# Second attention: forget sums and low queries in one product, value parts in one weight tile per head

## The reference

```python
log_f = jax.nn.log_sigmoid(f_logit + b_forget)
cum_log_f = jnp.cumsum(log_f, axis=1).transpose(0, 2, 1)
z = einsum('bhtd,bhsd->bhts', q, k) / 8 + cum_log_f[..., t] - cum_log_f[..., s]
z = where(s <= t, z, -1e30)
y_b = einsum('bhts,bhsd->bhtd', softmax(z), v)
y_b = (y_b * silu(z_b)) @ w_o_fox
```

## Time and profile before

| | before |
|---|---|
| median of 3 runs | 1290.13 us (1289.41 to 1290.8) |
| profiled execution, span from first to last instruction | 1286.8 us |
| TensorE busy | 1254.0 us (97%) |
| VectorE busy | 758.9 us (59%) |
| ScalarE busy | 586.3 us (46%) |
| GpSimd busy | 748.3 us (58%) |
| mean granted TensorE clock | 0.996 |

### The profile page before, as it was taken

One profiled execution on the slowest core, in us unless ns is written; L12 is line 12 of the kernel. 1 busy time (PEld: TensorE's weight loads), 2 busy tenths in 40 slices (PEclk: granted clock), 3 DMA queues, 4 the chain that ended last, 5 costly groups with the idle time before them and its releaser, 6 DMA issues.

```text
span 1286.8 us, 17060 instructions
## 1 busy us (share of the span) xinstructions
PE 1254.0 (97%) x6226; PEld 1044.0 (81%) x6226; DVE 758.9 (59%) x1245; ACT 586.3 (46%) x956; POOL 748.3 (58%) x863
## 2 busy tenths in 40 slices
PE   5999999999999999999999999999999999999997
PEld 4777878878888888887778988887888888888887
DVE  5868778334444367698787337754367616651565
ACT  3375667445664446233456644434333313331332
POOL 2644443434333676676545878535659957885782
PEclk9999999999999999999999999999999999999999
DMA  9412223222344733233224444212323333333322
GB/s 381 173 66 79 93 82 140 86 95 99 107 130 135 242 120 99 82 99 103 68 68 158 138 148 131 81 52 66 98 65 99 112 102 98 98 99 99 90 90 66
DMA packets 43107, 142.74 MB, mean 111 GB/s; under 512 B 4880, under 2 KB 7440, under 8 KB 41872
## 3 DMA queue, kind: packets, MB, share of 16 engines
q1 hardware_dynamic: 42768, 141.39, 33.6%
q10 hardware_dynamic: 256, 0.26, 0.1%
HBM read 130.88 MB, written 8.39 MB: 108 GB/s over the span
## 4 chain that ended last, share of the span: by engine, by line
PE 79%; DVE 14%; ACT 4%; issue 1%; POOL 1%; DMA 1%; SPq 0%; DVEq 0%; ACTq 0%; POOLq 0%
PE ps L124 78%; DVE tm L134 2%; DVE tm L137 2%; ACT tm L131 2%; ACT L131 1%; DVE ac L137 1%; PE ps L128 1%; DVE spl L134 1%; DVE tm L142 1%; DVE sph L145 1%; DVE x L137 1%; DVE ewl L134 1%; DMA x<-xin 1%; DVE ma L137 1%; POOL ycl L134 0%
## 5 line engine op out<-in xcount | busy, mean ns | idle before, releaser
L134 POOL TENSOR_TENSOR wl<-raw,wh 128x256 fp32r<-128x256 f32 x804 | 691.3, 892 | 480.6 <-ACT wh L131 472.7
L131 ACT ACTIVATE wh<-raw 128x1024 fp32r<-128x1024 f32 x201 | 212.0, 1055 | 310.8 <-PE ps L124 304.9
L124 PE MATMUL ps<-hh,wh 128*128 128x512 f32 x872 | 344.4, 395 | 0.0
L124 PE MATMUL ps<-hh,wl 128*128 128x512 f32 x872 | 340.2, 390 | 0.0
L124 PE MATMUL ps<-hl,wh 128*128 128x512 f32 x872 | 339.9, 390 | 0.0
L124 PEld LDWEIGHTS ps<-hh,wl 128*128 128x128 f32 x872 | 163.9, 188 | 34.9
L124 PEld LDWEIGHTS ps<-hh,wh 128*128 128x128 f32 x872 | 164.2, 188 | 33.3 <-DVE tm L137 0.4
L124 PEld LDWEIGHTS ps<-hl,wh 128*128 128x128 f32 x872 | 164.2, 188 | 32.9
L134 DVE TENSOR_TENSOR tm<-tm,tm 128x512 f32<-128x512 f32 (+4 forms) x113 | 94.3, 839 | 42.1 <-ACT tm L131 38.9
L137 DVE SCALAR_TENSOR_TENSOR tm<-cb,par_sb,tm 128x512 f32<-128x512 f32 x88 | 87.1, 990 | 50.5 <-ACT tm L131 47.1
L131 ACT ACTIVATE tm<-tm 128x512 f32<-128x512 f32 (+3 forms) x109 | 54.0, 531 | 80.5 <-DVE tm L137 64.5
(11 more groups left out here) (308 smaller groups left out, 2273.5 us busy)
## 6 DMA issues: line engine op xcount, KB each, us to landing
raw<-units SPq DMA_DIRECT2D x201, 512.0 KB, 3.5
ada<-units SPq DMA_DIRECT2D x16, 512.0 KB, 14.5
kept<-ge SPq DMA_DIRECT2D x16, 256.0 KB, 2.5
tm<-kept SPq DMA_DIRECT2D x16, 256.0 KB, 3.5
tm<-gate_w SPq DMA_DIRECT2D x12, 256.0 KB, 4.0
x<-xin SPq DMA_DIRECT2D x2, 1024.0 KB, 6.1
x<-xin SPq DMA_DIRECT2D x1, 2048.0 KB, 9.5
out<-x SPq DMA_DIRECT2D x16, 128.0 KB, 1.8
```

The source lines that it names most:

```text
L124: return self.none if self.e is None else self.e.matmul(out, lhs, rhs, start=start, stop=stop, skip_group_check=skip)
L131: return self.none if self.e is None else self.e.activation(out, in_, func, **kw)
L134: return self.none if self.e is None else self.e.tensor_tensor(out, a, b, op)
```

## The change

The one-hot rows move into the zero half of QL0, and the forget sums into a copy of the keys: KF[x] holds on one half the high keys of the head, and on the other the forget sums (high parts in 8 rows, low parts in 8 rows 32 further) and zeros. The second score product takes KF for K2, and the third is gone. VectorE writes the one-hot half behind the low queries and copies the keys behind their low parts. GpSimd zeroes both KF tiles in place of FT, later than FT was, as they lie in the first attention's value tiles.

The values of a head stand in one weight tile of 128 columns, 64 high and 64 low. Two passes, by PTh and PTl, give four parts; the result has the high values' half on partitions 0 to 63 and the low values' half on 64 to 127. ScalarE copies the latter to FO (`low_half`, last in its work for the head), VectorE adds it to the other half into the head's own half of the bank, and the gate product follows.

```diff
@@ constants @@
-        out[64 + h, o + h] = 1.0
+        for r in (32, 64, 96):
+            out[r + h, o + h] = 1.0
@@ tiles @@
+    KF = [at(f"kf{x}", [P, T], F32R, a1 + 4096 + 8192 * x + 6144) for x in range(2)]
+    VB = at("vb", [P, 4, 2 * T], F32R, vb0)
-    FT = at("ft", [P, T], F32R)
+    FO = at("fo", [64, T], F32)
+    def heads(tile, t, part):
+        return tile[:, t, :].rearrange("p (h x d) -> p h x d", h=8, x=2)[:, :, part, :]
+    def per_head(bank):
+        return bank[:, :].rearrange("p (h d) -> p h d", h=8)
@@ tensor_program, qk_b @@
+            pe.wait_ge(s_kf, c, x)
+            pe.wait_ge(s_hot, c, x)
...
-                pe.mm(PS[b][:, 0:n], QL0[p][x][:, w], K2[p][x][:, 0:n], False, False)
-                pe.mm(PS[b][:, 0:n], conr[0:72, CO + h:CO + h + 1].to_broadcast([72, 128]), FT[0:72, 0:n], False, False)
+                pe.mm(PS[b][:, 0:n], QL0[p][x][:, w], KF[x][:, 0:n], False, False)
@@ pv_b @@
-                vh, vl = (x[:, j, c * 128:(c + 1) * 128] for x in (VBh, VBl))
+                both = VB[:, j, 128 * h:128 * h + 128]
                 pe.wait_ge(s_vl, "b", j)
-                pe.mm(PS[b][:, 128 * j:T], vh, PTh[:, j, 128 * j:T], j == 0, False)
-                pe.mm(PS[b][:, 128 * j:T], vh, PTl[:, j, 128 * j:T], False, False)
-                last = pe.mm(PS[b][:, 128 * j:T], vl, PTh[:, j, 128 * j:T], False, j == 3)
+                pe.mm(PS[b][:, 128 * j:T], both, PTh[:, j, 128 * j:T], j == 0, False)
+                last = pe.mm(PS[b][:, 128 * j:T], both, PTl[:, j, 128 * j:T], False, j == 3)
@@ scalar_program @@
-                            act.wait_ge(l_mout[t // 2], 0)
+                            act.wait_ge(l_mout[0], 0)
+                            act.wait_ge(l_mout[1], 0)
...
+                        elif br == "b":
+                            act.fn(heads(VB, t, 0), per_head(PS[2 + t]), ACT.Copy).then_inc(*s_vh.up(br, t))
...
+        def low_half(h):
+            if h:
+                act.wait_ge(s_fold, h - 1)
+            act.wait_ge(s_pv, "b", h)
+            act.fn(FO[:, :], PS[6 + h % 2][64:128, :], ACT.Copy).then_inc(*s_half_out.up(h))
...
             gate(h + 8)
+            low_half(h)
@@ vector_program @@
+                elif br == "b":
+                    split_low(heads(VB, t, 1), per_head(PS[2 + t]), heads(VB, t, 0), (br, t), s_vl)
...
+        def key_copy(c, x):
+            own = HALVES[x][0]
+            dve.wait_ge(s_kh, "b", c, x)
+            if c:
+                dve.wait_ge(s_z, "b", 2 * c - 1, 0)
+            dve.cp(KF[x][own, :], K2[c % 2][x][own, :]).then_inc(*s_kf.up(c, x))
... in qk_low
+                    if br == "b":
+                        h = 2 * c + x
+                        dve.cp(QL0[p][x][other, :],
+                               conr[other, CO + h:CO + h + 1].to_broadcast([64, T])).then_inc(*s_hot.up(c, x))
...
+                    if br == "b" and c:
+                        key_copy(c, x)
... in gate_y
+            if br == "b":
+                dve.wait_ge(s_half_out, h)
+                o = PS[6 + h % 2]
+                dve.tt(o[r:r + 64, :], o[0:64, :], FO[:, :], ALU.add).then_inc(*s_fold.up(h))
+                dve.wait_ge(s_fold, h)
... forget sums
-        dve.wait_ge(s_fz, 0)
+        dve.wait_ge(s_fz, "keys")
-        dve.cp(FT[0:8, :], f1).then_inc(*s_fd.up("fh"))
+        dve.cp(KF[1][0:8, :], f1).then_inc(*s_fd.up("fh"))
+        dve.cp(KF[0][64:72, :], f1).then_inc(*s_fd.up("fh0"))
...
-        dve.cp(FT[64:72, :], f0).then_inc(*s_fd.up("ft"))
+        dve.cp(KF[1][32:40, :], f0).then_inc(*s_fd.up("fl1"))
+        dve.cp(KF[0][96:104, :], f0).then_inc(*s_fd.up("ft"))
+        for x in range(2):
+            key_copy(0, x)
@@ pool_program @@
-        pool.zero(f32(FT[:, :])).then_inc(*s_fz.up(0))
...
+            if name == ("f", 0):
+                pool.wait_ge(s_pv, "a", 7)
+                for x in range(2):
+                    last = pool.zero(f32(KF[x][:, :]))
+                last.then_inc(*s_fz.up("keys"))
             refill(name)
```

More of the change, by code:

```diff
@@ L423, in build @@
     s_fz, s_fd, s_fa, s_fp = sig("s_fz"), sig("s_fd"), sig("s_fa"), sig("s_fp")
+    s_hot, s_kf, s_half_out, s_fold = sig("s_hot"), sig("s_kf"), sig("s_half_out"), sig("s_fold")
     s_bias, s_pe, s_rc, s_pn, s_dn = sig("s_bias"), sig("s_pe"), sig("s_rc"), sig("s_pn"), sig("s_dn")
@@ L779, in pv_b @@
         def pv_b(h):
-            c, b = h // 2, 6 + h % 2
+            b = 6 + h % 2
             take(b)
@@ L1521, in scalar_program @@
         act.fn(TM[0][0:8, :], TM[0][0:8, :], ACT.Ln, bias=1.0).then_inc(*s_fa.up("ln"))
-        vproj("b", "bv", VBh)
+        vproj("b", "bv", None)
         def qk_b(h):
@@ L2144, in vector_program @@
         dve.ts(f1, PS[1][0:8, :], -1.0, ALU.mult).then_inc(*s_fd.up("f"))
-        dve.wait_ge(s_fz, 0)
+        dve.wait_ge(s_fz, "keys")
         dve.wait_ge(s_fd, "f")
-        dve.cp(FT[0:8, :], f1).then_inc(*s_fd.up("fh"))
+        dve.cp(KF[1][0:8, :], f1).then_inc(*s_fd.up("fh"))
+        dve.cp(KF[0][64:72, :], f1).then_inc(*s_fd.up("fh0"))
         dve.wait_ge(s_fd, "fh")
-        dve.tt(f0, f1, f32(FT[0:8, :]), ALU.subtract).then_inc(*s_fd.up("fl"))
+        dve.tt(f0, f1, f32(KF[1][0:8, :]), ALU.subtract).then_inc(*s_fd.up("fl"))
         dve.wait_ge(s_fd, "fl")
-        dve.cp(FT[64:72, :], f0).then_inc(*s_fd.up("ft"))
+        dve.cp(KF[1][32:40, :], f0).then_inc(*s_fd.up("fl1"))
+        dve.cp(KF[0][96:104, :], f0).then_inc(*s_fd.up("ft"))
+        for x in range(2):
+            key_copy(0, x)
         def top(key, k, b, n):
@@ L2185, in gate_add @@
                     dve.stt(o, t[:, :], pcol("c", k), o, ALU.mult, ALU.add).then_inc(*s_mod.up(*key))
-        v_low("b", VBh, VBl)
+        v_low("b", None, None)
         qk_b(0)
```

## The result

The changed kernel takes 1299.76 us (median of 5 executions, 1299.42 to 1300.09) against 1289.49 us for the kernel before, measured beside it (1288.89 to 1290.8): ratio 1.0074, 95% interval 1.0063 to 1.0085. The forecast was 1293.0 with a range to 1296.6. The direction and the waits came as forecast; the time lies 6.8 us above it. The profiled execution has a span of 1298.0 us and a mean granted clock of 0.989; before it was 1286.8 us and 0.996.

A forecast was written before the change was run, and what follows sets the result against it. TensorE's queue was taken as the bound. Saved passes, head 0 and waits: -10.4 + 0.3 + 2.4 + 3.9 + 3.6 + 1.6 = +1.4 us; clock +1.5; 1290.1 + 2.9 = 1293.0 us, range 1287.0 to 1296.6.

The forecast's parts named there:

- Removed passes: Second attention on TensorE: two passes fewer for each of eight heads, 0.65 us each, saving 10.4 us.
- The link: Chain from gate unit through ScalarE's late copy and VectorE's queue to low parts; TensorE resumes at g+7.8 for head 6.
- g: End of the gate unit on TensorE, equal to the start of the next head's transposes; the forecast counts times from it.
- rival (e): GpSimd blocks each slowed VectorE step for a whole subtraction, 0.87 us: +4.5 us over five links, 1297.5 us; chance 0.03.
- The waits: TensorE late behind VectorE's queue: heads 2 and 4 +2.4 us together, head 6 +3.9, head 7 +3.6, row sum +1.6.
- Head 0: First banks are released later by extra VectorE casts and key copies; half of the 0.65 us saved there lost, +0.3 us.
- The fold: VectorE's addition of the copied low half into PSUM, claimed to take 0.69 us like the gate product.
- Rival (c): The fold is dear, up to 1.4 us: each of five links 0.7 later, +3.5 us, 1296.5 us; chance 0.10.
- (d): Gaps between TensorE's products cancel the saving for half of the passes: 5.2 us, 1298.2 us; chance 0.02.
- The clock: One fall of TensorE's clock to half rate behind the two longest waits, +1.5 us; ends 0 and 3.0.
- (a): Links bind but cost less, no GpSimd slowing or clock fall: 1287.5 us; with slowing, no fall, 1291.5; chance 0.27.
- (b): The fold and its wait are hidden, only head 0's loss left: 1280.0 us; chance 0.12.

The follow-up runs named there:

- copy-early kernel: Changed kernel with ScalarE's copy of the low half moved ahead of the silu and the gate unit's bias and weight split: 1280.37 us, ratio 0.9929.
- filled kernel: Changed kernel with 16, 15 and 6 dummy products in TensorE's waits before head 7's scores, head 7's values and the row sum: 1290.88 us, ratio 1.0009.
- forget part alone: Changed kernel with the values' part undone (three value passes, no low-half copy, no fold), forget sums still in the low queries' product: 1284.79 us, ratio 0.9958.
- values' part alone: Changed kernel with the forget part undone (72-row product back), values' high and low parts still in one weight tile: 1303.67 us, ratio 1.0101.
- row sums first: Changed kernel with VectorE's two row sums per head placed ahead of its gate step, late copy left in place: 1288.06 us, ratio 0.9971.
- row sum filled: Changed kernel with 6 dummy 128x512 products in the wait before the row sum's one-column products alone: 1296.10 us, ratio 1.0041.
- head 6's wait filled: Changed kernel with 16 dummy 128x512 products in the wait before head 7's score products alone: 1295.92 us, ratio 1.0037.

## Why the prediction was wrong, step by step

**Removed passes: right.** The score block of head 3 in the changed kernel, 322.04 to 323.76, is 1.72 us and the value block to 325.07 is 1.31 us (2.28 and 1.95 before; forecast 1.6 and 1.3). The first product behind the wait has a pitch of 0.30 us in place of 0.23, 0.07 of the 0.12 us that 1.72 has over 1.6. The copy-early kernel shows the sum.

**The link: right to 0.1 us.** With g = 387.94 for head 6, ScalarE (gate bias, weight split, copy) and VectorE:

```profile
388.14 0.69 ACT L132 ACTIVATE ge<-ps,par_sb 128x512 f32<-128x512 f32 x1 [2.89 <-PE ps L125]
388.73 1.05 ACT L132 ACTIVATE wh<-raw 128x1024 fp32r<-128x1024 f32 x1
389.80 0.59 ACT L132 ACTIVATE fo<-ps 64x512 f32<-64x512 f32 x1
```

```profile
390.50 0.70 DVE L135 TENSOR_TENSOR ps<-ps,fo 64x512 f32<-64x512 f32 x1 [9.70 <-ACT fo L132]
391.23 0.69 DVE L135 TENSOR_TENSOR sz<-ps,sz 64x512 f32<-64x512 f32 x1
391.96 0.43 DVE L146 CAST vah<-sz 128x512 fp32r<-128x512 f32 x1
392.42 1.09 DVE L135 TENSOR_TENSOR val<-sz,vah 128x512 fp32r<-128x512 f32 x1
393.44 0.74 DVE L138 SCALAR_TENSOR_TENSOR ma<-tm,par_sb,ma 128x512 f32<-128x512 f32 x1
394.10 0.74 DVE L138 SCALAR_TENSOR_TENSOR ma<-gt,par_sb,ma 128x512 f32<-128x512 f32 x1
394.87 1.69 DVE L135 TENSOR_TENSOR ptl<-ps,pth 128x512 fp32r<-128x512 f32 x4
```

The copy starts at g+1.86 (forecast g+1.74), the low parts at g+6.93 (g+7.0), and TensorE at g+7.77 (g+7.8). Inside it two errors cancel: copy, fold, gate step and row sums together come some 0.3 us later, and the cast beside GpSimd wasn't slowed, 0.43 us in place of 0.81. The low part was slowed, 1.09 us here and 1.105 on the mean of four. GpSimd's row for it:

```profile
389.94 3.02 POOL L135 TENSOR_TENSOR wl<-raw,wh 128x256 fp32r<-128x256 f32 x4 [1.70 <-ACT wh L132]
```

It covers the cast (391.96 to 392.39) and half of the low part. It is made of four subtractions, and these say more (GpSimd's spans are rough): one ends at 392.06, the next at 392.96. The cast starts 0.10 us before an end and isn't longer; the low part starts 0.54 us before one and is 0.40 us longer. In the first attention of the kernel before, the cast at 208.19 starts 0.53 us before the end of a subtraction and is 0.38 us longer. So each step was held for no more than what was left of the subtraction that ran as it began. The Trainium skill (SBUF — State Buffer, "Who interferes with whom") calls the shared port pair an exclusive lock, on which whoever comes second fully blocks. The rows agree with that; they don't agree with rival (e), which made of it a whole subtraction for each step.

**The waits: right.** The profile's idle time ends at the modelled end of the product before, so the delays are taken from starts, as in the forecast (0.23 us from one product to the next). Heads 2 and 4: 322.04 - 320.59 - 0.23 = 1.22 us each, forecast 1.2. Head 6: 395.71 - 391.56 - 0.23 = 3.92, forecast 3.9. Head 7: the lag grows from 0.22 to 3.58 us, 3.36, forecast 3.6. Row sum: it grows from 4.44 (417.26 less 412.82) to 5.98 us, 1.54, forecast 1.6. Head 0, taken at 0.3, lost 0.45 of its score pass of 0.65: from the last product ahead of its scores to its transposes it is 276.27 to 284.15 us, before 276.08 to 284.16, only 0.20 less. Sum: 0.45 + 2.44 + 3.92 + 3.36 + 1.54 = 11.7, forecast 11.8.

**The fold: right.** It read 0.70 us, as the gate product beside it. Rival (c) is out; (d) is out by the sum of the copy-early kernel; (e) is out by the cast and the low part.

**The clock: this step failed.** The prediction says "I count one such fall, +1.5 us; the ends are 0 and two, 3.0". There were four, worth 8.9 us. Three things were wrong in it. It took the price from the one stretch of the earlier trace rows, 3 us at half clock, while the falls behind the new waits lasted 3.4 and 6.8 us; half of 6.8 us is 3.4, of which 2.6 showed, because the first 1.3 us of that fall lay still inside the wait. It looked only at the two waits above 3.5 us and passed over the row sum's, which stands directly before 16 one-column products. And its upper end was two falls at the price of the shortest, so the range had no case for what happened. Of the 7.4 us between 8.9 and the 1.5 in the sum, 2.6 are the two long waits (2.6 + 1.5 less 1.5), 3.2 the row sum's fall and 1.6 the fall near 517 us. The Trainium skill (TensorE: Matmul & The Clock Gate, Part 1: The HAM clock gate) ties the clock to recent activity; both long waits did bring a fall, as by that rule, at 4.1 us together in place of the 3.0 the prediction gave it.

That the delays sum so well owes something to luck: in the link two errors cancel, and head 0 is 0.15 us above its forecast while head 7 is 0.24 below.

The rivals: (a) and its 1291.5 with no fall is what the filled kernel shows (1290.88); (b), the hidden fold at 1280.0, is what the copy moved forward gives (1280.37).

**What stays open.** The fall near 517 us of the changed kernel has no wait in front of it: the 16 one-column products at 514.57 stand there in the kernel before too (505.34), at full clock. Of the five kernels with the late copy that were profiled afterwards, two have no fall behind 435 us (both fills of the head 6 wait), and the others have one near 695 us, or 702, or 506 and 690. Those near 690 to 702 stand behind a wait that the change doesn't touch, here in the kernel before and, behind the dots, in the one with the forget part alone:

```profile
687.37 0.36 PE L124 MATMUL ps<-ath,v2h 128*128 128x256 f32 x1 [1.67 <-DVE atl L134]
...
682.00 0.36 PE L125 MATMUL ps<-ath,v2h 128*128 128x256 f32 x1 [1.66 <-DVE atl L135]
```

It stands in all ten profiled kernels. In four the clock falls within 2 us behind it (forget part alone, values' part alone, row sums first, row sum filled), in the other six it doesn't. So the same wait brings a fall in one profile and none in the next. That speaks for chance in the fall near 517 too, but doesn't show it: all five executions of the changed kernel took 1299.42 to 1300.09 us at mean clocks of 0.988 to 0.990, so each of them lost about as much as the profiled one.

**Two readings of the prediction that carried nothing.** It put 3.3 us outside the span. In every execution with both numbers it is 1.7 to 2.2 us (1299.76 against 1298.0), so the profiled execution of the kernel before took some 1289 us (an estimate) and was one of the faster ones. And the earlier trace rows gives 17.95 us of products for a head in the middle; head 6 has 9.8.

## What to carry to other kernels

An instruction added to an in-order queue costs what stands in front of it there and delays what is queued behind it on the engine that waits: write the copy that another engine needs ahead of the unit whose products it doesn't depend on, and look at the order before the length. On an engine that runs without gaps a wait of some microseconds can be paid twice, once as time and once in the clock behind it: in the changed kernel's profile 3.8, 3.5 and 1.4 us of waiting brought 2.6, 1.5 and 3.2 us more. When a wait is forecast, count every fall that could follow it as a case, also for a short wait: here one of 1.4 us, with 16 one-column products behind it, had a fall, and one of 1.67 us had one in four profiles of ten.

## What the runs showed of the hardware

- A wait of 1.39 us with 16 products of 128x1 behind it had a fall to clock 0.50 for 6.8 us in the changed kernel, and one of 1.31 us, in the kernel with head 6's wait filled, for 3.4 us. Waits of 1.06 and 1.05 us before the 512-column products of heads 2 and 4 left the clock at 1.00, and so did 16 such products without a wait in the kernel before (505.34).
- A wait of 1.67 us, the same in all ten profiled kernels, had a fall close behind it in four of them and none in six.
- Work of no use can shorten a kernel: 37 dummy products in three waits took 8.9 us off.
- The clock's falls are not the same in each execution: with waits of 2.4 and 1.7 us, twelve executions went from 1283.9 us at 0.996 to 1292.1 us at 0.987, about 0.9 us for each thousandth. In the kernel before, sixteen beside them went from 1289.27 (0.996) to 1293.89 us (0.991).
- VectorE adding a PSUM and an SBUF operand of 64x512 into PSUM takes 0.70 us; multiplying two such operands into SBUF takes 0.69.
- A VectorE subtraction of two SBUF operands that began 0.54 us before the end of a GpSimd subtraction took 1.09 us in place of 0.69; a cast that began 0.10 us before such an end took 0.43, as with GpSimd idle.
